# Encoder trunk with experts on one core: routing beside the last output projection, first gather's inputs by VectorE, gate and up rows p, 128+p, 256+p

## The reference

```python
for layer in range(DEPTH):
    h = rmsnorm(x, mix_norm_g[layer])
    x = x + mixer(h, cos, sin, w_in[layer], ...)        # attention and short convolution, then w_out
    h = rmsnorm(x, ffn_norm_g[layer])
    x = x + (swiglu(h, ...) if layer % 2 == 0 else moe_swiglu(h, ...))
return rmsnorm(x, final_norm_g)

# moe_swiglu: d_ff 3584, 8 experts
logits = t @ w_router
top_val, top_idx = lax.top_k(logits, 2)
gates = softmax(top_val)
out = sum over e of combine[:, e:e + 1] * swiglu(t, w_gate[e], w_up[e], w_down[e])
```

## Time and profile before

| | us |
|---|---|
| median of three executions | 1375.39 |
| lowest, highest | 1372.77, 1375.85 |
| the profiled execution | 1375.52 |
| its span in the trace | 1373.6 |

### The profile page before, as it was taken

One profiled execution on the slowest core, in us unless ns is written; L12 is line 12 of the kernel. 1 busy time (PEld: TensorE's weight loads), 2 busy tenths in 40 slices (PEclk: granted clock), 3 DMA queues, 4 the chain that ended last, 5 costly groups with the idle time before them and its releaser, 6 DMA issues.

```text
span 1373.6 us, 20457 instructions
## 1 busy us (share of the span) xinstructions
PE 1299.1 (95%) x8939; PEld 813.1 (59%) x8939; DVE 556.4 (41%) x811; ACT 444.7 (32%) x664; POOL 9.6 (1%) x33
## 2 busy tenths in 40 slices
PE   7989999998986799899899999999999999999997
PEld 6777788877775567576765574743333354333343
DVE  5674455546575555555475483421000001200002
ACT  6554444436552445444345372410000000000001
POOL 2000000000000000000000000000000000000000
PEclk9999999999998799999999999999999999999999
DMA  9334455364000999999999999999999999999992
GB/s 335 111 123 184 184 185 188 116 245 158 27 0 16 359 398 397 383 372 403 401 404 409 388 409 404 399 408 409 408 409 400 370 370 360 367 388 403 407 396 100
DMA packets 128986, 418.74 MB, mean 305 GB/s; under 512 B 4176, under 2 KB 8304, under 8 KB 128896
## 3 DMA queue, kind: packets, MB, share of 16 engines
q1 hardware_dynamic: 127824, 416.30, 78.2%
q0 software_dynamic: 512, 1.12, 0.3%
q10 hardware_dynamic: 560, 0.01, 0.0%
HBM read 416.36 MB, written 1.05 MB: 304 GB/s over the span
## 4 chain that ended last, share of the span: by engine, by line
PE 88%; DVE 6%; ACT 3%; DMA 2%; issue 1%; DVEq 0%; ACTq 0%; SPq 0%
PE bank L1921 27%; PE bank L1617 14%; PE bank L1992 13%; PE bank L1619 13%; PE bank L1618 13%; PE bank L1859 2%; DMA ring<-in_moe_w_down 2%; PE bank L1853 2%; PE bank L1940 2%; ACT raw_d L743 1%; DVE lo L1043 1%; DVE mx L1132 1%; DVE raw_d L1129 1%; PE bank L1667 1%; PE bank L1726 1%
## 5 line engine op out<-in xcount | busy, mean ns | idle before, releaser
L1446 DVE TENSOR_TENSOR w_lo<-ring,w_hi 128x1024 fp32r<-128x1024 f32 x168 | 202.4, 1223 | 65.6 <-ACT w_hi L683 57.1
L1921 PE MATMUL bank<-ring,late_acts 128*32 128x256 f32 (+3 forms) x1936 | 215.8, 434 | 0.0
L683 ACT ACTIVATE w_hi<-ring 128x1024 fp32r<-128x1024 f32 x168 | 175.2, 1059 | 97.0 <-PE bank L1619 85.8
L1617 PE MATMUL bank<-hi,act_hi 128*128 128x512 f32 (+1 forms) x400 | 157.3, 393 | 13.4 <-DVE lo L1043 7.0
L1921 PEld LDWEIGHTS bank<-ring,late_acts 128*32 128x32 f32 (+1 forms) x1936 | 85.7, 120 | 121.6 <-issue 100.8
L1992 PE MATMUL bank<-ring,at_buf 128*32 128x256 f32 (+1 forms) x1408 | 157.1, 450 | 0.5 <-ACT at_buf L683 0.5
L1618 PE MATMUL bank<-lo,act_hi 128*128 128x512 f32 (+1 forms) x400 | 154.6, 387 | 0.0
L1619 PE MATMUL bank<-hi,act_lo 128*128 128x512 f32 (+1 forms) x400 | 154.4, 386 | 0.0
L683 ACT ACTIVATE at_buf<-bank 128x256 f32<-128x256 f32 (+2 forms) x40 | 18.0, 449 | 414.4 <-PE bank L1940 414.4
L1043 DVE TENSOR_TENSOR lo<-raw_gu,hi 128x1024 fp32r<-128x1024 f32 x96 | 112.4, 1221 | 28.1 <-ACT hi L683 27.4
L1468 DVE TENSOR_TENSOR silu_buf<-silu_buf,bank 128x512 f32<-128x512 f32 (+2 forms) x56 | 29.3, 536 | 226.8 <-PE bank L1921 193.4
(11 more groups left out here) (227 smaller groups left out, 1271.3 us busy)
## 6 DMA issues: line engine op xcount, KB each, us to landing
ring<-in_moe_w_up SPq DMA_DIRECT2D x50, 2048.0 KB, 14.9
ring<-in_moe_w_gate SPq DMA_DIRECT2D x49, 2048.0 KB, 13.6
ring<-in_moe_w_down SPq DMA_DIRECT2D x49, 2048.0 KB, 14.9
raw_gu<-in_w_in SPq DMA_DIRECT2D x7, 2048.0 KB, 13.0
ring_after<-in_moe_w_gate SPq DMA_DIRECT2D x7, 2048.0 KB, 13.1
ring_after<-in_moe_w_down SPq DMA_DIRECT2D x7, 2048.0 KB, 17.3
ring_after<-in_moe_w_up SPq DMA_DIRECT2D x6, 2048.0 KB, 15.5
raw_gu<-in_dense_w_gate SPq DMA_DIRECT2D x5, 2048.0 KB, 8.0
```

Of the source, the lines that this page charges most:

```text
L683: return nc.scalar.activation(out, in_, ACT.Copy, **kw)
L1446: v.tensor_tensor(w_lo[:, n % WP, :], flat(u)[:, q * 1024:(q + 1) * 1024], w_hi[:, n % WP, :], ALU.subtract).then_inc(w_lo_done, 1)
L1617: mm(out, ah, wh, start=start, stop=False, **kw)
L1921: ins = mm(bank[b][c * g.n:(c + 1) * g.n, 0:width], acts[STEPS[s][0]][:, k, g.col:g.col + g.n], by_rows(u, n)[:, kl, c * width:(c + 1) * w ...
```

## The change

1. **Routing.** The features are on the partitions as 128k+p. The router's weights `rout` hold 32 columns for each k (8 used), times the norm's weights, which a transpose of `g_route` brings to the partitions. x itself is turned (`route_turn`), the first half of its features in the middle of out1, and goes to `xT_route` by ScalarE (tile 0) and VectorE (tile 1). Four k run side by side in 32 columns of the array (`route_logits`); a product with `fold` adds the four groups and turns the result. No part is split. The choice of the two largest is made on logits without `rstd`; `rstd` comes in with the gates' exponential and with the selection (`build_sel`, now `is_equal` times `rstd`).
2. **Counting.** `down_part` and `eights` put 8 times the count plus 7-e into one bank, of which two products remain after `chosen`; the three for the slots follow (`slots_done`).
3. **out1's last piece** goes by token tile, so that tile 0 is added to x (`last_half`) while tile 1 is still multiplied.
4. **Rows for the gather** are x times the norm's weights, four products of VectorE on halves (`gained`), two after each half of the projection.
5. **SyncE** loads an expert's number when its first load needs it (`expert(r)`); the first unit comes as four DMAs of 512 KB with semaphores of their own (`first_in`).
6. **First steps.** `build_sel(0)` stands ahead of the gates' arithmetic and of the branch; first gather's copies and the first two pieces of unit 0 alternate on ScalarE and VectorE; `build_gsel(0)` and `build_sel(1)` follow the pieces of units 0 and 1. `experts_by_size` and the last norm stand directly behind the branch.
7. **Weights.** Gate and up rows are split as `(k p)`: partition p reads features p, 128+p, 256+p and so on.

```diff
-        eg_v = eg.rearrange("l e (p k) n -> (l e) p k n", k=KT)
-        eu_v = eu.rearrange("l e (p k) n -> (l e) p k n", k=KT)
+        eg_v = eg.rearrange("l e (k p) n -> (l e) p k n", k=KT)
+        eu_v = eu.rearrange("l e (k p) n -> (l e) p k n", k=KT)
...
-            experts = [sp.value_load(order[0:1, r:r + 1], min_val=0, max_val=NE - 1) for r in range(NE)]
+            loaded = {}
+
+            def expert(r):
+                if r not in loaded:
+                    loaded[r] = sp.value_load(order[0:1, r:r + 1], min_val=0, max_val=NE - 1)
+                return loaded[r]
...
+                    if u == 0:
+                        for q in range(4):
+                            sp.dma_start(by_rows(0, n)[:, q, :], w_v[e, :, q, f0:f0 + n]).then_inc(first_in[q], 16)
+                        continue
...
-                with act.If(over_size > 0):
+                with act.If(over_size < 1):
+                    experts_by_size()
+                    last_norm()
+                with act.Else():
                     experts_of_any_size()
-                with act.Else():
-                    experts_by_size()
+                    last_norm()
...
-                mix_pieces(layer, "out1", (6, 7), 0, 4)
+                if layer == 0:
+                    mix_pieces(layer, "out1", (6, 7), 0, 4)
+                else:
+                    mix_pieces(layer, "out1", (6, 7), 0, 2)
+                    tr(bank[GAIN][:, 0:KT], g_route[:, :], ident[0:KT, 0:KT]).then_inc(g_turned, 1)
+                    route_turn(0, 0, 10)
+                    route_turn(0, 1, 10)
+                    mix_pieces(layer, "out1", (6, 7), 2, 3)
+                    pe.wait_ge(router_ready, 1)
+                    for t in range(NT):
+                        route_logits(0, t)
+                    mm(bank[KEY][:, 0:NE], eights[:, :], down_part[:, :], start=True, stop=False)
...
+            def route_logits(c, t):
+
+                if t == 0:
+                    pe.wait_ge(route_x_act, c + 1)
+                else:
+                    pe.wait_ge(route_x_dve, c + 1)
+                for g in range(4):
+                    k = 4 * c + g
+                    ins = mm(bank[LOGIT_T[t]][32 * g:32 * g + 32, 0:P], rout[:, k, :], xT_route[:, k, t, :],
+                             start=c == 0, stop=c == 1)
+                return ins
...
+                for t in range(NT):
+                    route_turn(1, t, 11 + t)
+                for t in range(NT):
+                    route_logits(1, t).then_inc(logT_done, 1)
+                for t in range(NT):
+                    pe.wait_ge(logT_out, t + 1)
+                    mm(bank[LOGITS[t]][:, 0:NE], logT[:, t, :], fold[:, :], start=True, stop=True).then_inc(logits_done, 1)
...
+                mm(bank[KEY][:, 0:NE], eights[:, :], chosen[:, 0, :], start=False, stop=False)
+                mm(bank[KEY][:, 0:NE], eights[:, :], chosen[:, 1, :], start=False, stop=True).then_inc(rank_done, 1)
...
             def build_sel(p):
...
                         ins = v.tensor_scalar(sel[:, t, a:a + CAPS[r]], iota[:, 0:CAPS[r]], slot_r[:, t, r:r + 1],
-                                              None, ALU.is_equal)
+                                              rstd[:, t:t + 1], ALU.is_equal, ALU.mult)
...
                 pe.wait_ge(sel_done, 1)
+                pe.wait_ge(xg_done, 4)
                 for c in range(4):
-                    gather(0, c, c).then_inc(first_gather, 1)
-                pe.wait_ge(first_lo, 4)
+                    gather(0, c, FIRST_BANKS[c]).then_inc(first_gather, 1)
```

More of the change, by code:

```diff
@@ L483, in build_trunk @@
         order_done = sem("order_done")
+        first_in = [sem(f"first_in{q}") for q in range(4)]
         ring_in = [sem(f"ring_in{n}") for n in range(SLOTS_AFTER)]
@@ new lines, in route @@
+                v.tensor_tensor(at_rank[:, :, :], key.unsqueeze(1).to_broadcast([P, NE, NE]),
+                                keys[:, :].unsqueeze(2).to_broadcast([P, NE, NE]), ALU.is_equal)
+                dve.wait_ge(slots_done, 1)
+                ranks = bank[RANKS][:, 0:NT * NE].rearrange("p (t e) -> p t e", t=NT)
+                link(v.scalar_tensor_tensor(out=rank1[:, :, :], in0=ranks, scalar=1.0, in1=chosen[:, :, :].bitcast(F32),
+                                            op0=ALU.add, op1=ALU.mult))
@@ L1339, in route @@
+                link(v.tensor_scalar(slots[:, :, :], rank1[:, :, :], 1.0, None, ALU.subtract))
+                for t in range(NT):
+                    ins = v.tensor_tensor(picked[:, 0, t], at_rank[:, :, :],
+                                          slots[:, t, :].unsqueeze(1).to_broadcast([P, NE, NE]), ALU.mult)
                 link(ins)
-                v.tensor_tensor(chosen[:, :, :], oneh[:, 0], oneh[:, 1], ALU.add).then_inc(chosen_done, 1)
-                dve.wait_ge(gexp_done, 1)
+                link(v.tensor_reduce(slot_r[:, :, :], picked[:, 0], AX, ALU.add))
@@ new lines, in route @@
+                mm(bank[KEY][:, 0:NE], eights[:, :], chosen[:, 0, :], start=False, stop=False)
+                mm(bank[KEY][:, 0:NE], eights[:, :], chosen[:, 1, :], start=False, stop=True).then_inc(rank_done, 1)
+                r, to = bank[RANKS], [chosen[:, t, :].bitcast(F32) for t in range(NT)]
+                mm(r[:, 0:NE], before[:, :], to[0], start=True, stop=True)
+                mm(r[:, NE:2 * NE], ones[:, :], to[0], start=True, stop=False)
+                mm(r[:, NE:2 * NE], before[:, :], to[1], start=False, stop=True).then_inc(slots_done, 1)
```

335 lines of the change are left out of this document (194 added, 141 removed).

## The result

| | before | after |
|---|---|---|
| median, us | 1374.53 | 1360.83 |
| lowest, highest, us | 1372.77, 1375.85 | 1357.71, 1364.25 |
| profiled execution, us | 1375.52 | 1361.95 |
| its span, us | 1373.6 | 1360.5 |

The ratio is 0.990, with a 95% interval of 0.987 to 0.993: 13.7 us faster, where 17.1 was forecast. The time lies in the range given; one step of the working is wrong, and two terms are missing.

What follows compares the result with a forecast made beforehand. Bound: arithmetic in the trunk, nearly full DMA and TensorE in the experts, with a chain between that leaves both empty. DMA's start 13.0 plus gaps 4.1 gave 17.1 us off 1375.5: 1358.4, range 1353 to 1366.5.

Steps and rivals of the forecast that it cites:

- Work put into out1: Middle of out1: added transposes, router products and `down_part` take TensorE 2.0 us, so out1 ends at 429.6, not 427.6.
- The chain after out1: From out1's end to the order of the experts: 5.5 us instead of 16.6, the order 9.1 us sooner.
- Loading the expert numbers: SyncE ahead of the first weight load: one number instead of eight saves 3.9 us; first load 13.0 us sooner.
- First gather and first products: Start of the experts: gather from 439.5, branch charged 3.84 us, first product at 447.0, 16.2 us sooner.
- Weights by rows p, 128+p: Gate and up loads: new row split costs nothing, bounds -1.7 to +1.7 us.
- What the expert stage does with it: Experts ahead of 700 us: DMA's 13.0 us and 4.1 of closed gaps make the stage end 17.1 us sooner.
- 4.1 for gaps: Expert stage ahead of 560: DMA idle gaps of 0.9, 1.0 and 2.2 us close as TensorE frees units sooner.
- 400 GB/s or more up to 560: Sign for the forecast in the changed profile: DMA rate in the expert stage, where stretches had 372, 370 and 320.
- both rivals: The near rivals for the whole time: nothing recovered, 1362.5 us, chance 0.15; all gaps recovered, 1355.4 us, chance 0.2.
- nothing recovered: Rival, expert stage: slots come free too late, only DMA's 13.0 us start is gained; 1362.5 us, chance 0.15.
- Slower rows: Rival, gate and up loads: the new rows slow them; at 10% 20 us slower, 1395.5 us; chance 0.04.
- a longer chain: Rival, out1 to first load: order only 6 us sooner, number load's fixed cost 2 us; 1365.5 us, chance 0.12.

Runs made afterwards that it cites:

- the last experiment: The kernel before, with expert numbers loaded one at a time and the usual branch's code directly behind the branch: 1373.2 us, ratio 0.9993.
- again: The kernel after, unchanged, run once more beside the follow-up kernels: 1361.74 us, ratio 0.9911 to the kernel before.

## Why the prediction was right or wrong

*Work put into out1*: 2.0 us, and out1's end at 429.6. It ended near 427.7, which is this after the trunk's 2.05. Right.

*The chain after out1*: 5.5 us forecast, 5.8 measured. Right, and with it that the order comes about 9 us sooner: 10.8 with the trunk's 2.05, 8.8 without.

*Loading the expert numbers*: 3.9 forecast, 3.85 in the profile of after, 3.8 with seven numbers put back. Right: there is no fixed part worth speaking of. The estimate by the Trainium skill (DMA: Bandwidth & Descriptors, Latency and other measured facts), 600 ns for each, gave 4.2; these runs show 0.55 each, a little under that floor.

*First gather and first products*: 16.2 forecast, 18.0 measured without the trunk's part. The branch was charged in full, 3.84; it left VectorE idle for 1.5 us. The prediction named this ("an unchanged gap of 3.8 us at the branch says that its place does not matter"): its place does matter, and what it costs hangs on which code follows directly and on whether the weight loads already run. VectorE's idle time was 1.4 to 1.5 with the usual code directly behind the branch, 3.85 with the other code between and the weight loads not started, 7.0 and 6.6 with the other code between and the weight loads under way.

*Weights by rows p, 128+p*: nothing forecast, nothing measured (full stretches of 406 to 411 GB/s with either rows). Right.

*What the expert stage does with it* is the step that failed. It said that the wait at 567 shrinks since the gaps ahead of 560 close, and that "after the waits that end at 567 and 632 the two stand as before against each other, with the DMA as the later". Three things stand in its place.

First, what decides at the start. In the kernel before it was TensorE, as the last experiment shows; the DMA had about 4.5 us to spare at the first down unit (17.1 - 12.6). The traces show nearly this by another way. In the kernel before that unit left when a slot came free,

```profile
488.44 8.03 SPq L603 DMA_DIRECT2D ring<-in_moe_w_down  x2
```

and landed 10.6 us later, at 499.0, 6.6 us ahead of its product at 505.65. After, the chain of waits has

```profile
466.28 17.90 DMA ring<-in_moe_w_down
```

so it landed at 484.18, and the product followed 2.4 us later, at once. The difference of the two, 4.2, is what the DMA had to spare; the landings themselves lie 14.9 us apart, near the 14.65 of the DMA's start. After, it is the DMA that decides, as this row and the kernel that holds TensorE back show. The product came 17.1 us sooner without the trunk's part: the DMA's 12.6 and the 4.5 that it had to spare. That this is the forecast figure is a coincidence: the forecast had 13.0, and 4.1 for gaps.

Second, the waits near 550 and 616 did not shrink. The loads that they are for leave when TensorE frees a slot, and the DMA engines were far from full just before (8 GB/s from 551 to 552 in the kernel before, 143 from 534 to 535 in after), so they did not stand behind other loads, and no earlier start of the DMA could bring them forward. The chain of waits of after has

```profile
535.53 12.01 DMA ring<-in_moe_w_down
...
601.33 12.19 DMA ring<-in_moe_w_down
```

where the earlier trace rows have 11.99 and 11.88. A slot comes free when TensorE is done with it, and 12 us later the next weights are there, however early the whole stage began. The gaps that the forecast closed are partly there still: busy time by stretch of after has

```profile
530.00:540.00 10.00, 10.00 (x144) 5.92 (x142) 2.13 (x4) 0.38 (x1) 0.00 (x0) 1.00 0.90 346
...
590.00:600.00 10.00, 10.00 (x105) 6.89 (x108) 3.95 (x5) 1.06 (x1) 0.00 (x0) 1.00 0.76 289
```

That is 1.6 us of empty transfer ahead of the first of the two waits, where it was 4.1, and with 363 GB/s from 600 to 610 it is 4.1 ahead of the second, where it was 3.0. The forecast's sign of 400 GB/s or more up to 560 did not come. TensorE's lead went on falling, whatever the DMA had gained.

Third, two terms were missing. The new wait at 486 and the earlier ones leave TensorE at a lower granted clock than before in three stretches, 4.3 us of full-speed work; that this costs time is shown by the zeros multiplied in the waits, which kept PEclk at 1.00 in all five stretches and gave 5.6 us back in the median. And the usual branch's code, put first, must jump over the other at the end: 1.6 us of the span, about 1.1 of the time. The diff moved the branches, but the prediction costed that only at the start.

The ledger of the two spans, in us sooner: DMA's start 12.6, its slack at the first down unit +4.5, low clock -4.3, end -1.6, trunk +2.05; 13.25, and the spans differ by 13.1. The trunk's part is scatter and not the change's, which leaves 11.1 of the span for the change in this pair of executions; in the medians the gain is 13.7, and 12.5 for "again". The executions of one kernel lie up to 7 us apart, and no run says which share of this the trunk has. So the forecast of 17.1 was high by 3.4 to 6, and that the time lies in the range owes something to a range that reached up to both rivals.

One reading was wrong without harm: "After 700 us TensorE never waits". It waits 1.33 us at 749.92, and as long at 735.19 in after.

*The rivals*: "nothing recovered", 1362.5, is the nearest in number, and its reason, slots that come free too late, is what held the waits near 550 and 616. But its sum is not what happened either: more than the DMA's 13.0 was won ahead of 486, and the low clock and the end took it away again. Slower rows, and a longer chain, did not come.

## What to carry to other kernels

With a ring of a few load buffers, an earlier start of the loads moves the waits as they are: a wait is the time from a free slot to landed data (12 us here) less the work that is left meanwhile. More slots, smaller units or an earlier release should shorten it; none of these was tried here. Before counting a head start as a gain, find out for each of the two sides (loads, arithmetic) how much it had to spare at the first place where they meet; the cheap test is to hold one of them back on purpose. After every wait of some us in a full TensorE, read the clock of the stretch behind it: here it was worth about 5 us, and zeros multiplied during the wait gave it back. It also hides what a quicker start is worth: TensorE's 5 us seemed worthless as long as they ended in a wait with a low clock behind it, and 2.0 of them counted once the clock was kept up.

## What the runs showed of the hardware

A branch has a price that no row names, read only as idle time "<-issue" and as packets of the instruction queues. To code directly behind it VectorE is idle for 1.4 to 1.5 us with the load of the flag, and no such packet appears; to code behind all of the other branch's it is 3.85, with five of them from 446 to 450; 7.0 and 6.6 when the weight loads already keep all DMA engines busy. That instruction packets appear at such a branch, and that it takes about 3 us longer beside running loads, agrees with the Trainium skill (Runtime: NRT & Kernel Launch, Instruction fetch mechanics), by which a taken branch whose target lies outside of the prefetched window has to fetch it by DMA first. A jump over the unused branch's code costs wherever it stands: 2.45 us ahead of the last norm (3.02 where 0.57 stands without it), 1.6 of the span at the program's end.

TensorE's granted clock was 0.59 to 0.80 in the 7 us behind waits of 2.8 to 4.2 us, in the same places in both runs of the kernel after, while in the kernel before the stretch behind a wait of 2.77 us (at 678.03) had 1.00, and with TensorE held back so had the one behind 2.87 us (at 615.49), so the length of the wait alone does not tell it. With zeros multiplied in the waits it was 1.00 at all five.

Loads of a number from the order into a register on SyncE stand one behind another, 0.55 us each (seven of them put the first DMA off by 3.8), and no DMA that is issued behind them leaves before the last.
